# Two layers with experts on one core: four row tiles lent as weight slots, norm scaling on ScalarE, row tiles first in the queue

## What is computed

```
def rms_norm(x, g, eps=NORM_EPS):
    y = x * lax.rsqrt(jnp.mean(x * x, axis=-1, keepdims=True) + eps)
    return y * g
...
for i in range(DEPTH):
    hp_n = rms_norm(hp, norm_mix[i]); hs_n = rms_norm(hs, norm_mix[i])
    # layer 0: sliding window attention with sinks; layer 1: differential attention
    hp = hp + yp; hs = hs + ys
    hp = hp + hier_moe(rms_norm(hp, norm_ffn[i]), ...)   # top group, then top 2 of its 8 experts
    hs = hs + hier_moe(rms_norm(hs, norm_ffn[i]), ...)
y_prompt = rms_norm(hp, norm_final); y_sample = rms_norm(hs, norm_final)
```

## Time and profile before

| | |
|---|---|
| median of 3 runs | 1202.94 us (1199.99 to 1203.72) |
| profiled execution | 1204.02 us, of which the span is 1202.2 |
| TensorE busy | 1049.9 us, 87% |
| VectorE, ScalarE, GpSimd busy | 428.6, 215.5, 283.0 us |
| moved by DMA | 279.01 MB, mean 232 GB/s |
| chain that ended last | TensorE 68%, DMA 20%, VectorE 4%, SP's queue 3% |

### The profile page before, as it was taken

How to read it: one execution, slowest core, us unless ns; L and a number is a source line. 1 busy time by engine, 2 the same in 40 slices (tenths; PEclk the granted TensorE clock), 3 DMA queues, 4 the chain that set the end, 5 groups by cost and what they waited for, 6 DMA issues and landing times.

```text
span 1202.2 us, 17948 instructions
## 1 busy us (share of the span) xinstructions
PE 1049.9 (87%) x6864; PEld 748.9 (62%) x6864; DVE 428.6 (36%) x1364; ACT 215.5 (18%) x677; POOL 283.0 (24%) x445
## 2 busy tenths in 40 slices
PE   5999999969999788839999999999997999988860
PEld 4877778955555455528667686777884555545430
DVE  2235454342332222252242433435553234222226
ACT  2124441110000000011122233223300000000001
POOL 2513331021232121122021221221202322212213
PEclk9999999979999999969999999999988999999995
DMA  9222042368999999974321302144158999999965
GB/s 317 73 78 106 2 176 111 157 228 320 370 379 381 384 381 388 390 276 150 105 82 36 116 29 89 63 193 176 65 215 301 379 382 381 376 394 386 382 247 222
DMA packets 81240, 279.01 MB, mean 232 GB/s; under 512 B 9942, under 2 KB 36646, under 8 KB 63424
## 3 DMA queue, kind: packets, MB, share of 16 engines
q1 hardware_dynamic: 63440, 231.75, 51.6%
q0 software_dynamic: 15840, 34.92, 8.8%
q10 hardware_dynamic: 1872, 11.14, 2.5%
HBM read 265.51 MB, written 28.70 MB: 245 GB/s over the span
## 4 chain that ended last, share of the span: by engine, by line
PE 68%; DMA 20%; DVE 4%; SPq 3%; issue 2%; ACT 2%; POOL 1%; POOLq 0%; DVEq 0%; ACTq 0%
PE ps L1699 21%; DMA area<-in_w_up 16%; PE ps L1982 12%; PE ps L1691 10%; PE ps L1994 6%; PE ps L1966 3%; SPq L491 3%; PE ps L1707 2%; PE ps L2174 2%; DMA area<-in_w_a_qkv 1%; PE ps L1863 1%; PE ps L1675 1%; PE ps L2140 1%; PE ps L1878 1%; PE ps L1752 1%
## 5 line engine op out<-in xcount | busy, mean ns | idle before, releaser
L1982 PE MATMUL ps<-area 128*64 128x256 f32 x1040 | 254.5, 401 | 46.1 <-DMA area<-in_w_up 37.7
L1699 PE MATMUL ps<-area 128*128 128x256 f32 x1152 | 266.5, 385 | 3.6 <-issue 2.0
L1983 PE MATMUL ps<-area 128*64 128x256 f32 x1040 | 255.3, 402 | 0.0
L1699 PEld LDWEIGHTS ps<-area 128*128 128x128 f32 x1152 | 215.5, 192 | 34.6 <-issue 4.5
L1982 PEld LDWEIGHTS ps<-area 128*64 128x64 f32 x1040 | 144.8, 144 | 115.6 <-issue 54.8
L638 POOL DMA_INDIRECT y_scratch<-area,idx_i x64 | 65.0, 1015 | 374.6 <-DVE area L1414 331.1
L1983 PEld LDWEIGHTS ps<-area 128*64 128x64 f32 x1040 | 144.7, 144 | 0.0
L1994 PE MATMUL ps<-area 128*64 128x512 f32 x260 | 125.4, 604 | 1.1 <-DVE area L1407 0.8
L1399 DVE SCALAR_TENSOR_TENSOR area<-ps,area 64x256 f32<-64x256 f32 x64 | 31.4, 491 | 263.9 <-ACT area L909 263.9
L1995 PE MATMUL ps<-area 128*64 128x512 f32 x260 | 125.4, 604 | 0.0
L1691 PE MATMUL ps<-area 128*128 128x272 f32 x512 | 123.2, 395 | 0.0
(11 more groups left out here) (221 smaller groups left out, 1080.2 us busy)
## 6 DMA issues: line engine op xcount, KB each, us to landing
area<-in_w_gate SPq DMA_DIRECT2D x65, 1024.0 KB, 25.5
area<-in_w_up SPq DMA_DIRECT2D x65, 1024.0 KB, 25.7
area<-in_w_down SPq DMA_DIRECT2D x65, 1024.0 KB, 26.2
area<-in_w_b_qkv SPq DMA_DIRECT2D x12, 1024.0 KB, 7.9
area<-y_scratch ACTq DMA_DIRECT2D x8, 1024.0 KB, 8.0
area<-in_w_a_qkv SPq DMA_DIRECT2D x6, 1024.0 KB, 13.2
out<-area POOLq DMA_DIRECT2D x12, 512.0 KB, 3.5
area<-in_w_a_o SPq DMA_DIRECT2D x4, 1024.0 KB, 5.6
```

The source lines that it names most:

```text
L1699: ins = nc.tensor.matmul(ps[:r, bank, at_col:at_col + F], x[:, k, COL[t]:COL[t] + r], w[:, k, :], start=k == k0, stop=k == k1 - 1)
L1982: nc.tensor.matmul(ps[0:CAP, bank, 0:F], x[:, k, :], wg[:, k, :], start=k == 0, stop=k == KD - 1)
L1983: ins = nc.tensor.matmul(ps[CAP:P, bank, 0:F], x[:, k, :], wu[:, k, :], start=k == 0, stop=k == KD - 1)
```

## The change

- The ring gets two more slots, H1 and H0, at its end: `hid`'s tiles 2 and 3, and 0 and 1. They open when the rows are stored in DRAM, squared and transposed. After the last expert load SP reads the four tiles back from DRAM, and `combine` waits for that as well as for the results. With 21 slots, `OV_AFTER` and the steps around it move by two experts.
- `last_use` frees each slot of the out projection with the last product that reads it.
- For n = 0 and 2 the rows are multiplied with `rstd` on ACT (`root_rows`) instead of DVE, without the norm vector. The vector is applied after the transpose, in `xt_copy`: ACT in four copies with a scale by partition, DVE in one multiplication. It is now loaded transposed (4 KB) at the start for both layers, and only the last norm has a broadcast.
- SP issues the row loads: tiles 0 and 1 ahead of the key weights, the other three behind the value weights. The wait ahead of the query weights is gone.
- In layer 0 the key products of tiles 0 and 1 come ahead of their value products, and the later turns lie between them. In layer 1 only tile 0 is turned ahead of the first key product, and the turn of tile t + 1 stands between the key and the value product of tile t.
- Some semaphores are merged (`prepared`, `layer1_in`).

```diff
-OV_AFTER = 19
+OV_AFTER = 21
-MOE_SLOTS = [["N0", ..., "X0", "X1"]] * 2
+MOE_SLOTS = [["N0", ..., "X0", "X1", "H1", "H0"]] * 2
...
+        if name[0] == "H":
+            i = 2 * int(name[1])
+            return hid[:, i:i + 2, :].rearrange("p a b -> p (a b)")
...
         if x == "o":
-            return o_mm, OUT_BASE["ab".index(kind) + 1]
+            layer = "ab".index(kind)
+            return o_mm, OUT_BASE[layer] + 1 + max(n for n, item in enumerate(OUT[layer]) if item[1] is None or i in item[1])
...
+        if name[0] == "H":
+            return [(y_flip, NT * (2 * layer + 2)), (sumsq, NT * (2 * layer + 2))] + \
+                [(y_out[b], 16 * (3, 2)[b] * (layer + 1)) for b in range(2)]
...
+            for name in ("H1", "H0"):
+                sp.wait_ge(*last_use([key for key, at in MOE_LOADS[layer] if at == name][-1]))
+                for t in (2 * int(name[1]), 2 * int(name[1]) + 1):
+                    sp.dma_start(hid[:, t, :], hn_dram[COL[t]:COL[t] + P, :]).then_inc(tile_in[t], 16)
...
+        rows_in(0)
+        rows_in(1)
         for n, (key, name) in enumerate(A_LOADS):
-            if n == 2:
-                sp.wait_ge(tile_in[2], 16)
             load_after_owner(key)
+            if n == 1:
+                rows_in(2)
+                rows_in(3)
+                rows_in(4)
...
-        g_load(0, I["norm_mix"][0])
+        for l in range(2):
+            pool.dma_start(gT[:, 2 + l, :], I["norm_mix"][l].rearrange("(p k) -> p k", k=KD)).then_inc(g_in, 16)
...
+        def root_rows(n, i):
+            act.wait_ge(rstd_ready, NT * n + i + 1)
+            if i >= 2:
+                act.wait_ge(y_flip, NT * n + i - 1)
+            nc.scalar.activation(ynorm[n][i % 2][:r, :], hid[:r, t, :], ACT.Copy, scale=rstd[:r, t:t + 1]).then_inc(y_ready, 1)
...
+                for k in range(4):
+                    ins = nc.scalar.activation(xTn[n][:, k, COL[t]:COL[t] + r], ps[:, b, k * P:k * P + r], ACT.Copy,
+                                               scale=gT[:, 2 + n // 2, k:k + 1])
...
+                nc.vector.tensor_tensor(x, turned, g, ALU.mult).then_inc(xt_dve, 1)
...
-            dve.wait_ge(tile_in[t], 16 * (layer + 2))
+            dve.wait_ge(tile_in[t], 16 * (layer + 2) if t == 4 else 16 + 32 * (layer + 1))
...
+        k_a(0)
+        k_a(1)
+        v_a(0)
+        v_a(1)
+        flip_a(0)
+        flips(0, 2)
+        k_a(2)
...
         flips(2, 0)
-        flips(2, 1)
         for t in range(NT):
             copied(2, t)
             if t < 4:
                 position(pos_no(0, "K", t))
+                flips(2, t + 1)
                 position(pos_no(0, "V", t))
-            if t + 2 < NT:
-                flips(2, t + 2)
```

More of the change, by code:

```diff
@@ L257, in program, with slot @@
     slot_at.update({f"X{i}": R_X + SLOT * i for i in range(2)})
+    def slot(name):
+        if name[0] == "H":
+            i = 2 * int(name[1])
+            return hid[:, i:i + 2, :].rearrange("p a b -> p (a b)")
+        return part(slot_at[name], SLOT)
     oT = part(R_X, KD, N)
@@ L410, in weights @@
         name, value = WHERE[key]
-        return part(slot_at[name], SLOT), w_ready[name], value
+        return slot(name), w_ready[name], value
     def last_use(key):
@@ L673, in moe @@
                         overfull_scatter(0)
-                if e == NE - 3:
+                if layer and e == NE - 3:
                     with pool.If(extra > 0):
@@ L677, in moe @@
                     with pool.If(extra < 2):
-                        g_load(2 + 2 * layer, I["norm_final"] if layer else I["norm_mix"][1])
+                        g_load()
             with pool.If(extra > 1):
@@ L682, in moe @@
                     overfull_scatter(o)
-                wait_apart(pool, s["scat"], 16 * extra)
-                g_load(2 + 2 * layer, I["norm_final"] if layer else I["norm_mix"][1])
+                if layer:
+                    wait_apart(pool, s["scat"], 16 * extra)
+                    g_load()
         for i in range(NT):
@@ L837, in q_copy @@
                                  bias=bq[:, 2 * j + m:2 * j + m + 1]).then_inc(q_act, 1)
[L839 to L849, removed]
+        square(0, 0)
+        square(0, 1)
+        root_rows(0, 0)
+        root_rows(0, 1)
+        xt_copy(0, 0)
+        xt_copy(0, 1)
+        square(0, 2)
+        root_rows(0, 2)
+        square(0, 3)
+        xt_copy(0, 2)
+        root_rows(0, 3)
+        k_copy(0)
+        square(0, 4)
+        xt_copy(0, 3)
+        root_rows(0, 4)
+        k_copy(1)
         xt_copy(0, 4)
@@ L852, in _ @@
         k_copy(3)
+        act.wait_ge(bias_in, 48)
         q_copy(0, 0)
@@ L1085, in xt_copy @@
             dve.wait_ge(y_flip, NT * n + i + 1)
-            nc.vector.tensor_copy(xTn[n][:, 4:8, COL[t]:COL[t] + r],
-                                  ps[:, b, :].rearrange("p (k c) -> p k c", c=P)[:, :, 0:r]).then_inc(xt_dve, 1)
+            x, turned = xTn[n][:, 4:8, COL[t]:COL[t] + r], ps[:, b, :].rearrange("p (k c) -> p k c", c=P)[:, :, 0:r]
+            if n % 2:
+                nc.vector.tensor_copy(x, turned).then_inc(xt_dve, 1)
+            else:
+                if i == 0:
+                    dve.wait_ge(g_in, 32)
+                g = gT[:, 2 + n // 2, 4:8].unsqueeze(2).broadcast_to([P, 4, r])
+                nc.vector.tensor_tensor(x, turned, g, ALU.mult).then_inc(xt_dve, 1)
         def twice(x):
@@ L1795, in kv_a, with v_a, kv_sample_a @@
                 pe.wait_ge(kv_sb, t - 1)
[L1796 to L1805 removed]
+            rows_mm(4 + t % 2, 0, t, xTn[0], matrix(("a", "k", 0)))
+        def v_a(t):
+            if t == 0:
+                arrived(("a", "v", 0))
+            rows_mm(4 + t % 2, F, t, xTn[0], matrix(("a", "v", 0))).then_inc(kv_mm, 1)
+        def kv_sample_a():
+            copied(0, 4)
+            pe.wait_ge(kv_sb, 3)
+            sample_mm(4, xTn[0], [matrix(("a", "k", 0)), matrix(("a", "v", 0))]).then_inc(kv_mm, 1)
         def flip_a(i):
@@ L1834, in _ @@
         flips(0, 1)
-        for t in range(NT):
-            copied(0, t)
-            kv_a(t)
-            if t + 2 < NT:
-                flips(0, t + 2)
-            if t >= 1:
-                flip_a(t - 1)
+        k_a(0)
[5 more added lines that the diff above has]
+        k_a(2)
+        flips(0, 3)
+        v_a(2)
+        flip_a(1)
+        k_a(3)
+        flips(0, 4)
+        v_a(3)
+        flip_a(2)
+        kv_sample_a()
+        flip_a(3)
         q_a(0, 0, 0)
```

105 lines of the change are left out of this document (49 added, 56 removed).

## The result

| | before | after |
|---|---|---|
| median of 4 runs each | 1202.9 us (1199.99 to 1203.72) | 1190.51 us (1189.07 to 1195.13) |
| ratio, 95% interval | | 0.9911 [0.9896, 0.9926] |
| span of the profiled execution | 1202.2 us | 1192.9 us |
| mean granted clock | 0.952 | 0.946 |

What follows compares the result with a forecast made beforehand. Both expert stages were taken to end by transfers, with TensorE setting the pace elsewhere except at seams. Start -3.7, layer 0 -5.35, tail +1.0, seam -1.7, layer 1 -4.8 sum to -14.55: 1188.4 us, range 1181 to 1198.5.

Steps and rivals of the forecast that it cites:

- The slots: Expert stages: two more slots fill the DMA hole behind the first loads, 3.8 us in layer 0, 3.9 in layer 1.
- the rival that they bring nothing: Expert stages: the hole is start-up time of transfers, not missing slots; 1196.1 us, chance 0.17.
- far bound of -7.7 for layer 0: Expert stage of layer 0, slots and gather together: forecast -5.35 us, bounds 0 and -7.7.
- as in the rival: More gain than forecast: start -5.5, layer 0 -7.05, seam -2.7, layer 1 -6.4, tail +1.0; 1182.3 us, chance 0.12.
- Start: Kernel start: reordered loads let the first key product begin at 12.2 us; -3.7 us, bounds -1.5 and -5.5.
- Gather: Opening of expert stages: starts 0.8 us earlier in layer 0, lands 0.75 sooner there and 0.9 in layer 1.
- Tail of layer 0: End of layer 0's stage: row return hidden, layer 1's first loads beside scatter and read; +1.0 us, bounds 0 and +2.7.
- the slower rival: Both tails: the return of the rows is on the path, each tail growing by 11.5 us; 1210.4 us, chance 0.05.
- Seam: First combine to layer 1's first key product: only tile 0 turned first; -1.7 us, bounds 0 and -2.7.
- the turn (1.97, slow as before): Seam into layer 1: turn of tile 0 on TensorE taken at 1.97 us, ending at 535.3.
- signs named ahead: First key product near 12 us, DMA share above 0.95, landing under 3, return before last scatter, key product within 10.5.
- those that would have shown it wrong: Hole behind the first gather, first combine waiting for rows, or TensorE waiting for ScalarE's copies at more than one place.

Runs made afterwards that it cites:

- first pair: The kernel before and the changed kernel, each profiled in its first measurement: spans 1202.2 and 1192.9 us.
- second pair: Both kernels run and profiled once more, nothing edited: 1202.34 us before, 1190.24 us changed, ratio 0.9894.

## Why the prediction was right, and where it was not

**The slots** were the right mechanism, a little under-sized in layer 0: forecast 3.8 and 3.9, measured 4.3 to 5.8 and 3.6 to 4.3 between the kernels, 4.9 and 4.4 by the run without them. Both estimates took the 20 us window alone, filled at 381 and 384 GB/s (it fills at 388 to 398); where the rest of layer 0 comes from is not shown. The kernel without the two slots took 1197.3, near the 1196.1 priced for the rival that they bring nothing. The far bound of -7.7 for layer 0 does not follow from its terms (5.5 + 0.8 + 0.75 is 7.05, as in the rival); nothing hung on it.

**Start.** The row chain came out as worked (12.38 and 11.74 for 12.2; the copies 1.14, the root 1.15, the wait 1.23), but the key weights, put at 9.3 and so off the path, landed at 11.1 to 12.3, 9.4 to 10.6 us behind their issue, about when the turns end: that they cost at most 0.67 is luck. And the term lacked an entry: the key matmuls at half speed, 1.7 to 2.5 us before the change and 0.0 to 2.2 after. Their row was there, 32 products that begin at 17.23 and take longer than 32 of a later tile, and the forecast did not read it.

**Gather.** The slots given back one by one brought the forecast 0.7. The step that failed is the landing, taken as 2.7 from a scatter: it stayed at 3.39 to 3.47 in layer 0 and at 3.43 to 3.65 in layer 1, in every profile. In the changed kernel the DMA engines were busy 0.28 to 0.30 of that time, with 72 to 78 GB/s, which is the gather's own 0.26 MB; in the kernel before 0.41 to 0.64. So other traffic of this size is not what sets it, and 1.65 us of the forecast, both layers together, never came.

**Tail of layer 0.** Right in what and where, wrong in size: the loads that the ring puts behind the last expert cost 2.5 and 3.1, about the far bound of 2.7, where +1.0 was taken. That rows coming back would sit on the path, the slower rival, did not happen: the last of the four reads, issued at 488.9, landed within 18.7 us, ahead of the scatter at 508.99, and the first combine waited for results. With the loads moved away and the rows where they were, the scatter took 2.63. What acted is the rival's mechanism, transfers of another queue beside the scatter, with weights in place of rows.

**Seam.** The step that failed is "the turn (1.97, slow as before)": the clock was counted for the turn and then forgotten for the product behind it. The forecast also read the row at 537.23 as the turn of both tiles; it is tile 1's alone. Tile 0 was turned at 533.52, TensorE then waited 1.74, and the product followed tile 1's turn with no gap, 5.5 us behind the begin of the first turn; only its first 1.5 us ran at the low clock. After, TensorE makes one turn, waits 1.23 for copies, and the product begins 3.2 us behind that turn's begin and runs at 1.2 GHz for most of its length. The key product did start about 10 us behind the first combine, as forecast (12.6 before), and then lost 2.2 to 3.3 us against its 3.46 at 2.4 GHz.

**Sum.** Over-counted: landings 1.65, tail 1.5 to 2.1, seam 1.4 to 2.5, and in the first pair the 1.7 of the clock ahead of layer 1's gather. Under-counted: slots up to 2.4 (first pair; 0.2 in the second) and the start, 1.7 in the second pair. The range held, and for mostly the reasons given, but the closeness of 1188.4 to 1190.5 owes something to terms that cancelled. Of the signs named ahead, the first key product near 12, the DMA shares behind the first loads, the return ahead of the last scatter and the key product 10.0 us behind the first combine came; the gather's landing under 3 did not. None of those that would have shown it wrong came: the wait of 1.2 for copies in the seam is the one the forecast had counted in its path.

## What to carry to other kernels

When a ring of buffers gets longer, look where its last turn ends: the slots that the next stage fills first should be those that come free earliest, or its first loads land beside the last latency-bound transfers of this stage. A product that is started earlier by doing less ahead of it meets the clock that the pause before left; price it at that clock. And moving a load out of the way of one transfer brought nothing here when it then stood beside a larger one: what helped was to send it ahead, where its bytes fitted in.

## What was not expected of the hardware

- A gather of 64 rows of 4 KB took 3.39 to 3.65 us from issue to landing, with the DMA engines busy 0.28 of that time as well as 0.64.
- 1 MB of weights in packets of 1.0 KB took 12.8 to 17.25 us beside result reads in packets of 7.1 KB on another queue; the same load took 9.4 to 10.6 at the start, beside other loads of its own queue.
- 34 turns that compute nothing raised TensorE from 1.2 to 2.4 GHz ahead of the work that mattered, and took 2.7 to 3.8 us off the way to the first query product.
- The same program met different clocks at the same place: with TensorE busy throughout, the product ahead of layer 1's gather ran at 0.50 in one profile of the changed kernel and at 1.00 in the other, 1.7 us apart.
